# A chunked scan: blocks of two chunks stored and loaded ahead of the rest, transposes between copies, a state product on four quarters

## The reference

```python
def step(state, inp):
    r_t, w_t, k_t, v_t, kk_t, b_t = inp
    sa = jnp.einsum('bhij,bhj->bhi', state, kk_t)
    state = (state * w_t[:, :, None, :] - sa[..., None] * b_t[:, :, None, :]
             + v_t[..., None] * k_t[:, :, None, :])
    y_t = jnp.einsum('bhij,bhj->bhi', state, r_t)
    return state, y_t
```

## Time and profile before

| what | us |
|---|---|
| three runs, median (lowest, highest) | 1260.31 (1258.64, 1261.17) |
| the profiled execution, whole | 1260.45 |
| its span, first to last instruction | 1258.7 |
| busy in the span: PE, DVE, ACT, POOL | 1165.2, 752.7, 617.9, 484.8 |
| solver's steps and what stands between them, DVE | 216.6 to 280.7 |
| gate run's last product, PE | ends 290.84 |
| first corner to end of the last y | 300.65 to 386.07 |
| ACT: copy of 64x512 (w, u, y); of 64x256; gate tile; weight split | 0.59; 0.38; 0.58; 1.06 |
| DVE: copy of 64x512; mask of 64x256; state tile | 0.69; 0.42; 0.69 |

### The profile page before, as it was taken

The page is one execution under the profiler, slowest core; times in us unless marked ns, Lnnn a source line. Parts: engine busy times, 40 slices in busy tenths (PEclk is TensorE's granted clock), DMA queues, the critical chain, the costliest instruction groups (busy, mean ns, idle before and its releaser), DMA issues.

```text
span 1258.7 us, 19508 instructions
## 1 busy us (share of the span) xinstructions
PE 1165.2 (93%) x7570; PEld 901.6 (72%) x7570; DVE 752.7 (60%) x1179; ACT 617.9 (49%) x1018; POOL 484.8 (39%) x391
## 2 busy tenths in 40 slices
PE   5899899997886899899999998999999999999977
PEld 4665667676773687677777776777888888867656
DVE  4775996793556536566766656364285234567753
ACT  4667453633553336656656464364221244466655
POOL 1432334355760244323333334443444445532321
PEclk8999899998998899999999999999999999999988
DMA  6742245427005162221221222522333333222111
GB/s 235 251 113 67 68 102 149 131 88 194 12 4 172 34 191 85 84 67 56 77 67 55 67 84 68 165 86 69 99 100 90 96 100 101 84 76 60 52 33 67
DMA packets 198909, 119.49 MB, mean 95 GB/s; under 512 B 27741, under 2 KB 187174, under 8 KB 198566
## 3 DMA queue, kind: packets, MB, share of 16 engines
q1 hardware_dynamic: 197312, 116.08, 31.4%
q10 hardware_dynamic: 1510, 2.20, 0.5%
HBM read 103.06 MB, written 15.20 MB: 94 GB/s over the span
## 4 chain that ended last, share of the span: by engine, by line
PE 38%; issue 29%; POOL 15%; DVE 12%; ACT 2%; DMA 2%; SPq 0%; POOLq 0%; ACTq 0%; DVEq 0%
POOL b_w_lo L547 13%; PE banks L625 10%; PE banks L626 10%; PE banks L627 10%; DVE b_problems L2077 2%; DVE b_sum_squares L2075 1%; PE banks L1193 1%; DVE b_a_lo L1937 1%; PE banks L632 1%; PE banks L1221 1%; POOL b_sum_squares L592 1%; DVE b_sum_squares L2010 1%; DMA b_spread_heads<-spread_heads 1%; DVE b_suffix L2523 1%; POOL b_squares L584 1%
## 5 line engine op out<-in xcount | busy, mean ns | idle before, releaser
L547 POOL TENSOR_TENSOR b_w_lo<-b_w_raw,b_w_hi 128x512 fp32r<-128x512 f32 x320 | 428.9, 1361 | 717.3 <-ACT b_w_hi L1291 717.2
L625 PE MATMUL banks<-b_a_lo,b_w_hi 128*128 128x512 f32 x1280 | 525.0, 410 | 31.6 <-DVE b_a_lo L2190 12.7
L627 PE MATMUL banks<-b_a_hi,b_w_lo 128*128 128x512 f32 x1280 | 505.5, 395 | 0.0
L626 PE MATMUL banks<-b_a_hi,b_w_hi 128*128 128x512 f32 x1280 | 504.7, 394 | 0.0
L625 PEld LDWEIGHTS banks<-b_a_lo,b_w_hi 128*128 128x128 f32 x1280 | 243.8, 190 | 110.5 <-issue 26.1
L1291 ACT ACTIVATE b_w_hi<-b_w_raw 128x1024 fp32r<-128x1024 f32 x160 | 168.7, 1055 | 252.4 <-PE banks L627 247.0
L627 PEld LDWEIGHTS banks<-b_a_hi,b_w_lo 128*128 128x128 f32 x1280 | 243.7, 190 | 53.9
L626 PEld LDWEIGHTS banks<-b_a_hi,b_w_hi 128*128 128x128 f32 x1280 | 244.6, 191 | 44.6
L1682 ACT ACTIVATE b_exps<-banks,b_stats 128x128 f32<-128x128 f32 (+3 forms) x64 | 33.2, 524 | 60.1 <-DVE b_stats L2313 60.1
L1617 ACT ACTIVATE b_a_hi<-b_x_t,b_params 128x512 fp32r<-128x512 f32 x48 | 33.9, 719 | 54.7 <-DVE b_x_t L2198 54.2
L2198 DVE TENSOR_TENSOR b_x_t<-b_x_t,banks 128x512 f32<-128x512 f32 x32 | 21.9, 686 | 60.7 <-PE banks L627 60.7
(11 more groups left out here) (315 smaller groups left out, 1512.4 us busy)
## 6 DMA issues: line engine op xcount, KB each, us to landing
b_w_raw<-rw_w_in SPq DMA_DIRECT2D x32, 512.0 KB, 4.4
b_w_raw<-da_w_in SPq DMA_DIRECT2D x32, 512.0 KB, 4.0
b_w_raw<-w_in_a SPq DMA_DIRECT2D x32, 512.0 KB, 4.0
b_w_raw<-pe_w_gate SPq DMA_DIRECT2D x16, 512.0 KB, 4.1
d_ple<-b_ple_out SPq DMA_DIRECT2D x16, 256.0 KB, 4.9
b_w_raw<-rw_w_out SPq DMA_DIRECT2D x8, 512.0 KB, 6.6
b_ple_in<-d_ple SPq DMA_DIRECT2D x2, 2048.0 KB, 10.3
b_w_raw<-da_w_out SPq DMA_DIRECT2D x8, 512.0 KB, 4.0
```

The lines of the kernel that those rows point to most:

```text
L547: m = pool.tensor_tensor(WLO[:, u % 2, ks], WRAW[:, u, ks], WHI[:, u % 2, ks].bitcast(F32), ALU.subtract)
L625: pe.matmul(dst, hi, a_lo[:, k_act, :], start=first, stop=False)
L626: pe.matmul(dst, hi, a_hi[:, k_act, :], start=False, stop=False)
L627: return pe.matmul(dst, lo, a_hi[:, k_act, :], start=False, stop=last)
```

## The change

Nothing is computed otherwise; buffers, places and orders change.

- The stores are cut: first the 32 partitions of chunks 0 and 1 (`first_out`), then SP loads their blocks, then it stores the other 96 (`prob_in`). ScalarE issues the turned loads of the first pair, after gate tile 6, and splits the output's second weight tile after gate tile 7 instead of before it. The two weight loads come after all block loads.
- The blocks of chunks 0 and 1 have their own buffer (`TRI0`), as has each of the two states (`SV0`, `SV1`); `TURNED` moves to where `UV` will be, so that GpSimd's first placement in `UV` waits for the stores.
- Products of chunk 0: both halves without a wait between them (banks 0 and 1, 6 and 7); the waits on the gate tiles are taken one by one.
- `NKR` has two buffers; `rows_of(c+1, 0)` moves to before `u_of(c)`, `rows_of(c+1, 1)` to before `y_chunk(c)`; GpSimd scales rows first, then the state, then places kT and V.
- The corners go to banks 3 and 4, the first after `products(c+1, 1)`.
- `y_at(h, j)` changes the output half with every tile, so that four products in a row use the four quarters of TensorE; `keep_y` needs four copies of half the size for it.
- The bonus tiles 2, 3 and 4 move from the solver's steps 3, 5 and 10 to 5, 8 and 11.

```diff
+    TRI1, SV1 = phase([("blocks1", [P, NC - 2, NT, CH]), ("sv1", [P, NT, 2, CH])], dx_at)
+    XA, UV, SV0, TRI0 = phase([("x_a", [P, NT, 2, CH]), ("uv", [P, NT, 2, CH]), ("sv0", [P, NT, 2, CH]),
+                               ("blocks0", [P, 2, NT, CH])], tail_at)
...
+        sp.wait_ge(sem("inverse_done"), 1)
+        sp.dma_start(solved[0:head], prob[0:head]).then_inc(sem("first_out"), 16)
+        sp.wait_ge(sem("inverse_done"), 2)
+        sp.dma_start(turned[0:head], TURNED[0:head, :]).then_inc(sem("first_out"), 16)
+        sp.wait_ge(sem("first_out"), 32)
+        load_blocks(0, 2)
+        sp.dma_start(solved[head:P], prob[head:P]).then_inc(sem("prob_in"), 16)
+        sp.dma_start(turned[head:P], TURNED[head:P, :]).then_inc(sem("prob_in"), 16)
         sp.wait_ge(sem("prob_in"), 48)
...
+        load_blocks(2, 4)
+        load_turned(1)
+        load_blocks(4, NC)
+        out_weights(2, 4)
...
         place_v(in_sv(0), 0)
-        place_v(in_uv, 1)
         for u in range(2):
             low_part(RUN_RWO[0], u)
+        pool.wait_ge(sem("lo_done"), RUN_RWO[0] + 2)
+        pool.wait_ge(sem("prob_in"), 48)
+        place_v(in_uv, 1)
         for c in range(NC - 1):
+            if c + 2 < NC:
+                scale_nk(c + 1)
+            if c:
+                scale_state(c)
             place_kt(c + 1)
             place_v(in_sv(c + 1), 2 * c + 2)
-            if c:
-                scale_state(c)
-            if c + 2 < NC:
-                scale_nk(c + 1)
...
-        def y_at(h):
+        def y_at(h, j):
-            return YB[h][low if h == 0 else up]
+            return YB[h][(low, up)[(h + j) % 2]][:, tile_cols(j)]
...
         for g in range(2):
             products(0, g)
-            rows_of(0, g)
+        pe.wait_ge(sem("gate_kept"), NT - 1)
+        rows_of(0, 0)
+        pe.wait_ge(sem("gate_kept"), NT)
         first_corner(0)
+        rows_of(0, 1)
...
-            if more and c % 2:
-                first_corner((c + 1) // 2)
+            if c + 2 < NC:
+                rows_of(c + 1, 0)
             u_of(c)
             y_state(c)
             if more:
                 products(c + 1, 1)
+            if more and c % 2:
+                first_corner((c + 1) // 2)
+            if more:
                 s_of(c)
             if c + 2 < NC:
-                rows_of(c + 1, 0)
+                rows_of(c + 1, 1)
...
+            if j == NT - 2:
+                act.wait_ge(sem("first_out"), 32)
+                for n in range(2):
+                    for h in range(2):
+                        act.dma_start(TRT[block_rows(h, 0), n], D_TT[n, :, h].rearrange("j k s -> k j s")
+                                      ).then_inc(sem("turned_in"), 16)
...
-            if n == 3:
+            if n == 5:
                 bonus(2)
-            if n in (5, 10):
-                bonus(n // 5 + 2)
+            if n in (8, 11):
+                bonus(n // 3 + 1)
```

More of the change, by code:

```diff
@@ L460, in _ @@
         out_weights(0, 2)
[L461 to L465, removed]
+        solved, turned = D_T.rearrange("c j h s t -> (c j h) (s t)"), D_TT.rearrange("c j h k s -> (c j h) (k s)")
+        head = 2 * NT * 2
         def load_blocks(first, last):
             for c in range(first, last):
-                for h, hp in enumerate((slice(0, CH), slice(CH, P))):
-                    sp.dma_start(TRI[hp, c], D_T[c, :, h].rearrange("j s t -> s j t")).then_inc(sem(f"blocks_in{min(c // 2, 1)}"), 16)
+                for hp in (slice(0, CH), slice(CH, P)):
+                    sp.dma_start(blocks_of(hp, c, slice(0, CH)), D_T[c, :, hp.start // CH].rearrange("j s t -> s j t")
+                                 ).then_inc(sem(f"blocks_in{c // 4}"), 16)
         def load_turned(pair):
+            sp.wait_ge(sem("corner_mm"), 2 * pair - 1)
             for n in range(2):
@@ L866, in products @@
             n = 2 * c + g
[L867 to L868 removed]
+            xb = YB if n == 1 else XB
+            if n > 1:
+                pe.wait_ge(sem("x_kept"), 6 if n == 2 else 4 * n)
             for m4 in range(4):
@@ L872, in products @@
                 for rows_, even, odd in ((low, 0, 1), (up, 1, 0)):
-                    pe.matmul(XB[0][rows_, o], NKX[low, even, j, chunk(c)], kr[0], start=True, stop=True, skip_group_check=True)
-                    m = pe.matmul(XB[1][rows_, o], NKX[up, odd, j, chunk(c)], kr[1], start=True, stop=True, skip_group_check=True)
+                    pe.matmul(xb[0][rows_, o], NKX[low, even, j, chunk(c)], kr[0], start=True, stop=True, skip_group_check=True)
+                    m = pe.matmul(xb[1][rows_, o], NKX[up, odd, j, chunk(c)], kr[1], start=True, stop=True, skip_group_check=True)
             m.then_inc(sem("x_mm"), 1)
@@ L959, in y_chunk @@
             for j in range(NT):
-                for h in range(2):
-                    m = pe.matmul(y_at(h)[:, tile_cols(j)], UV[:, j, h, :], XR[:, c % 2, j, h, :], start=False,
-                                  stop=(j == NT - 1), skip_group_check=True)
+                for h in ((0, 1), (1, 0))[j % 2]:
+                    m = pe.matmul(y_at(h, j), UV[:, j, h, :], XR[:, c % 2, j, h, :], start=False, stop=(j >= NT - 2),
+                                  skip_group_check=True)
             m.then_inc(sem("yx_mm"), 1)
@@ L2141, in _ @@
             keep_strict(0, g)
+        dve.wait_ge(sem("corner_mm"), 1)
+        keep(TRT[block_rows(1, 1)].rearrange("p n j t -> p (n j t)"), BANK[3][block_rows(1, 1)], "corner_kept")
+        for g in range(2):
             keep_incl(0, g)
-        dve.wait_ge(sem("corner_mm"), 1)
-        keep(TRT[block_rows(1, 1)].rearrange("p n j t -> p (n j t)"), BANK[6][block_rows(1, 1)], "corner_kept")
         for c in range(NC):
```

124 lines of the change are left out of this document (66 added, 58 removed).

## The result

The changed kernel takes 1252.25 us (median of 7 runs, 1247.08 to 1255.32) beside 1260.52 for the kernel before on the same chip (7 runs, 1256.09 to 1261.83): a ratio of 0.9938, 95% interval 0.9917 to 0.9958. It is faster, by 8.3 us; the forecast was 16.6 us, and 1252.25 lies outside the range of 1240 to 1249.

What follows compares the result with a forecast made beforehand. No one engine but four successive chains bound the edited stretch: pre-scan solver waits, the solved blocks' DRAM round trip, chunks 0 to 5, and the tail. Gains 3.1+6.8+2.2+4.8-0.3 = 16.6 us gave 1243.9 us, range 1240 to 1249.

Steps and rivals of the forecast that it cites:

- The bonus tiles: Before the scan: moving them ends solver and gate run 3.1 us sooner, bounds 0 and 4.3.
- The head: Stores of chunks 0 and 1 land at about 284, their last block load at 289.3, first corner at 290.4.
- 32 partitions might use one DMA engine: Rival on the head's store: 0.5 MB take 25 us, landing at 307, time 1266 us; chance 0.04.
- the rest of the stores: Scan's start: 1.9 MB issued at 286.6 land at 293, up to 295.5; GpSimd's V placement and scaling wait behind.
- u of chunk 0: Scan's start: its term, from the gate run's end, gains 6.8 us; u starts at 297 to 299.
- the clock falls again: Rival: after a TensorE gap before chunk 1's rows, eight groups run at 1.2 GHz: 3.4 us lost, 1247.3; chance 0.16.
- the next term: u of chunk 0 to w of chunk 1: 5.3 us at full clock instead of 7.49, gain 2.2.
- The loop: w of chunk 1 to w of chunk 7: gain 4.8 us, bounds 0.5 and 6, despite five scaling stalls of 1.33.
- The slower scaling: Rival: GpSimd's scaling is slower beside VectorE, 0.85 us a chunk, 1248.2 us; chance 0.07.
- The state part: Output's state part on four quarters of TensorE: 0.45 us off each chunk, bounds 0 and 0.5.
- the tail: Chunk 7 and after: 0.45 gained, 0.35 lost in copies, 0.4 in loading x; together -0.3 us.

Runs made afterwards that it cites:

- e3: The changed kernel with bonus tiles 2, 3 and 4 at the solver's old steps 3, 5 and 10: 1255.61 us.
- e10: The kernel before with only the new bonus tile steps 5, 8 and 11: 1256.9 us, ratio 0.9978 to the kernel before.
- e7: e1 with a head of 64 partitions (four chunks) in place of 32: 1252.57 us.
- e6: The changed kernel with the rest of the stores issued only after the head's block loads have landed: 1253.38 us.
- e1: The changed kernel with TURNED in a free weight buffer, so GpSimd's first V placement needn't wait for the rest of the stores: 1247.9 us.
- e9: e1 with only the turned part of the rest stored after u of chunk 0: 1246.78 us, ratio 0.9894 to the kernel before.
- e4: The changed kernel with the output's state part on two quarters of TensorE again, as before: 1254.65 us.
- e8: e1 with the whole rest of the stores issued only after u of chunk 0: 1251.86 us.
- e2: The changed kernel with the rest of the stores issued before SP waits for the head and loads its blocks: 1250.52 us.
- e5: The changed kernel with the rest of each store sent as three transfers of 32 partitions: 1253.49 us.

## Why the prediction was wrong

**The bonus tiles** were right: 3.1 forecast, 3.5 in the profiles, 3.4 and 2.8 us in e3 and e10.

**The head** was right: it landed at 284.1 (start-up taken off) against 284. Its loads came a microsecond later than the 289.3 forecast, so the first corner waited 0.66 us, and still started at 290.4. The rival that 32 partitions might use one DMA engine is refuted (0.5 MB in 4.0 us), but it asked the right question, what a store from few partitions moves, and I asked it only of the head.

**The step that failed** is the one on the rest of the stores: "4.5 us of the 6.5 are for 2 MB, so 2 + 4.3 us, 293 if nothing is in its way, and up to 295.5". That scales a time by bytes. Its 1.9 MB took 10.1 us, longer than the 2.5 MB of before with 8.8, since 64 of its 96 partitions crowd one half of the places, just as in the whole store (e7, e6). That explains a time about as long as the whole's 8.8 us; the last 1.3 are open. It was issued when forecast (286.6; 288.66 is 286.8 with the start-up taken off). Landing at 298.74, 296.9 with the start taken off, is 1.4 us beyond the upper bound and 3.9 beyond the 293. On it hang u of chunk 0, 3.7 us short of its term (0.4 of them are its transposes at the low clock), and by the rival *the clock falls again* the next term too: the wait grew to 4.84 us, the clock fell to 0.50 and the 2.2 us from u of chunk 0 to w of chunk 1 were lost entirely. I had that rival at a chance of 0.16 and 3.4 us; a late landing is what makes the gap long, so the two should have been counted as one case. The forecast also had no term for TensorE's idle behind the stores: with the wait gone and the stores as they were, e1 still needs 11.48 us from the gate run to u of chunk 0. With most of both gone the terms come out: 9.66 us from the gate run to u of chunk 0 in e9 (forecast 297.1 less 287.7, 9.4) and 5.54 from there to w of chunk 1 (forecast 5.3).

**The loop**: 3.7 for 4.8. The mechanism is right, five stalls of 1.4 us (1.33 forecast), odd chunks 11.4 to 12.1 (11.5), chunk 6 7.7 (7.7). Mis-sized are the even chunks, 9.4 to 9.5 for 9.2, and one odd chunk of 12.14. The slower scaling is refuted: 1.9 us each time. **The state part** was right to 0.05 (e4), **the tail** right.

**The rest of the miss**: 10.6 us in the profiles are 8.3 in the medians. Between the two profiled executions the start-up accounts for it, as the one of after stood 1.9 us later: 10.6 less 1.9 is 8.7. Whether the other runs stood as late is not on record, so how much of the 10.6 the medians would show is open; their interval reaches from 5.3 to 10.5 us.

In sum: of the 6.0 us that the profiles lack, 3.7 are the late landing, 2.2 the clock that it brought down, 1.1 the loop, less 0.4 at the bonus tiles and 0.6 behind the group norm.

## What to carry to other kernels

When a store or load is split by partitions, price each part by the partitions in it and not by its bytes: here half of the bytes from half of the partitions took nearly as long as the whole, and the late end of such a transfer held a buffer that GpSimd and, behind it, TensorE needed. Before a buffer is laid over another, ask when the last transfer out of it lands; moving it to a free place was worth 4.4 us. And look at what stands behind a wait on the engine that waits: GpSimd's scaling stood behind a wait that it didn't need, and putting it ahead was worth 0.46%, 5.8 us, more than any other single edit tried here.

## What the hardware showed that was not expected

- At equal DMA share (1.26), a store from 32 partitions moves 262 GB/s and one from 128 moves 524; 64 partitions take 8.0 to 8.3 us for 1.25 MB, 128 take 8.8 us for 2.5 MB, with weight loads beside them.
- TensorE stood still for 2.75 us with no semaphore to wait for while two large stores were under way, 0.97 us with a smaller one, and not at all with none; a 16 KB instruction packet moved when the stores ended (e1, e9, e8).
- Where the scan begins the granted clock fell to 0.50 in or after waits of TensorE of 3.04 us (e10), 3.36 (e7), 3.66 (before), 4.84 (after), 5.75 (e2), 6.17 (e5), 7.61 (e6) and 8.19 (e8), and it stayed at 1.00 through the idle of 2.75 us in e1. The length of the wait alone doesn't decide: at 514 us it fell after 2.56 us in e7, and the same wait, 2.57 us, left it at 1.00 in the profiles of before and after.
